# The mLSTM core with tokens on partitions

## Chip, cores and metric

The kernel runs on one core of a Trainium2 chip. The time is the device time of one execution in microseconds; before the change three runs gave 1299.15 to 1300.79 us, median 1299.8. A core has a matmul engine (PE, with PEld for its weight loads), a vector engine (DVE), a scalar engine (ACT), GpSimd (POOL) and a queue for DMA (SP). Each works through its own list of instructions in order; they meet only at semaphores.

## The reference, cut to what matters

A trunk of two layers on 512 tokens of width 1024 in float32. Layer 0 mixes tokens by latent attention, layer 1 by an mLSTM with 8 heads (query and key 64 wide, values 128 wide); behind each stands a squared-ReLU MLP of width 4096. The change touches only the mLSTM mixer:

```
qk   = silu(conv(u @ W_qk));  v = u @ W_v;  gate = sigmoid(u @ W_o_gate)
ig   = 15 tanh((i_pre + i_b) / 15);  lf = log_sigmoid(15 tanh((f_pre + f_b) / 15))
for each head, token t and earlier token s <= t:
    w[t, s]  = exp(b[t] - b[s] + ig[s] - m[t])        # b: running sum of lf, m: running maximum
    S[t, s]  = (q[t] . k[s]) / 8 * w[t, s]
    num[t]   = sum_s S[t, s] v[s]                     # 128 values
    den[t]   = sum_s S[t, s]                          # row sum
    h[t]     = num[t] / max(|den[t]|, exp(-m[t]))
    h[t]     = h[t] / sqrt(mean(h[t]^2) + 1e-6) * head_gain
mixer out = (gate * h) @ W_out
```

The kernel computes the chunkwise recurrence in this closed form. Division and norm fold into one factor per head and token: `(mean(num^2) + 1e-6 * dd^2) ^ -0.5`, with `dd` the maximum above.

## The kernel before, in words

Every large product is made in three passes. A float32 operand is split into a high half (`hi`, a cast to fp32r, by ACT) and a low half (`lo`, the rest, by DVE or POOL), and `product` (L1460 to L1469) issues hi*lo, hi*hi and lo*hi. Activations lie transposed, features on partitions and 512 tokens in the free dimension, as 8 tiles `xh`/`xl` and 8 tiles `uh`/`ul`. Weights come as strips of 1024 x 256 through two slots (`raw`, `whi`, `wlo`): SP loads, ACT casts (L636), DVE or POOL forms the low half (L963, L516), PE multiplies. Four PSUM banks rotate for dense tiles (`RING`, `free_bank`).

The order of the work is written out by hand for each engine; nothing plans it at run time. Layer 1 goes: gate rows, then four times a query/key strip and a value strip. The value strips (L1787 to L1797) already have the tokens stationary: 128 tokens by 256 columns, two halves to a bank. Then come four strips `N_O` of the output gate (tiles `T_O` to `T_O + 7`) in the transposed form, with `tile`: DVE scales a tile by the row of norms (`scaled`, L1361), ACT takes the sigmoid (L936), POOL multiplies the head gain into it (`gain`, L586).

The core follows, one head per step, software-pipelined over the engines. `i` and `lead` name a head by pair and parity; heads 3 to 6 stand in a loop (`Fori`) on each engine. For a head, with four blocks of key tokens j (512, 384, 256, 128 query columns, the causal triangle):

- DVE copies the head's 64 key rows into a zeroed 128-row buffer (`k_copy`, L1312) and adds the causal mask to the row of maxima (`masked`, L1322), which SP has brought into all partitions (`mb`).
- PE forms scores, key tokens on partitions (`st_product`, L1809); ACT the exponentials (`weights`, L859), seven instructions a head; DVE multiplies the two (`weighted`, L1330); ACT casts the result (`high`, L876), POOL forms its low half (`head_parts`, L563).
- PE forms the numerator, 128 value dimensions by 512 tokens (`numerator`, L1823), and in 8 more matmuls against two columns of ones the row sums in one row (`row_sums`, L1839).
- ACT squares the numerator (L886) and copies the row of sums (L892). PE adds the squares over partitions and turns the row of sums, both into columns (`head_sums`, L1848). DVE makes the norm's argument (`head_norm`, L1363), POOL raises it to -0.5 (`head_pow`, L573), DVE puts it on a diagonal (`head_diag`, L1379), PE spreads that over all partitions (`norm_spread`, L1862), DVE multiplies by the gate and by the numerator (`gated`, L1386).
- ACT casts and DVE forms the low half (L896, L1396) into `uh`/`ul`, the input of the output projection, whose first strip runs on PE beside the last heads (`out_products2`, L1868). Then come the other three strips and the MLP of layer 1.

Some steps have two buffers, by parity of the head or of the block. The halves of the scores (`swh`, `swl`) and of the values (`mvh`, `mvl`) lie in `xh` and `xl`, which the gate projection still reads.

Of the kernel before, what the change touches and what calls it, by code (L numbers as in the profile page):

```python
# [5 lines left out]
F32 = mybir.dt.float32  # L6
# [62 lines left out]
B_ST, B_NUM, B_BCH, B_DEN, B_STAT = 4, (3, 7), 0, 2, 6  # L69
# [30 lines left out]
def trunk(nc, a, out):  # L100
    ctx = ExitStack()
    with ctx:
# [42 lines left out]
        stat = sb("stat", [P, 2, 8])  # L145
        den_row = acc[0:1, :]
# [61 lines left out]
        sg = C("sg", [P, MH, S])  # L208
# [5 lines left out]
        rb = C("rb", [P, 2, S])  # L214
        mkh = C("mkh", [P, 2, S], F32R)
        mkl = C("mkl", [P, 2, S], F32R)
        numsq = rb
# [12 lines left out]
        otmp = yc  # L230
# [13 lines left out]
        mvh = flat(xh)[:, 3072:4096].rearrange("p (t n) -> p t n", t=TT)  # L244
        mvl = flat(xl)[:, 3072:4096].rearrange("p (t n) -> p t n", t=TT)


# [6 lines left out]
        def bank(b):  # L254
            return ps[:, b, :]

# [27 lines left out]
        sig_new, sg_ready = sem("sig_new"), sem("sg_ready")  # L284
# [3 lines left out]
        mk_zero, den_mm, den_read = sem("mk_zero"), sem("den_mm"), sem("den_read")  # L288
        md_ready, mk_ready, mv_hi, mv_lo = sem("md_ready"), sem("mk_ready"), sem("mv_hi"), sem("mv_lo")
        st_mm, w_exp, sw_mul, sw_hi, sw_lo = sem("st_mm"), sem("w_exp"), sem("sw_mul"), sem("sw_hi"), sem("sw_lo")  # L290
        num_mm, num_sq, ms_mm, stat_read = sem("num_mm"), sem("num_sq"), sem("ms_mm"), sem("stat_read")
        var2_ready, rc2_ready, diag2_ready = sem("var2_ready"), sem("rc2_ready"), sem("diag2_ready")
        bc2_mm, rb_ready, hs_ready = sem("bc2_mm"), sem("rb_ready"), sem("hs_ready")
# [182 lines left out]
        def _(pool):  # L476
# [86 lines left out]
            def head_parts(i, lead, early=False):  # L563

                for j in range(TT):
                    z = 4 * lead + j
                    pool.wait_ge(sw_hi, i * 8 + (z + 1))
                    g.tensor_tensor(swl(lead % 2, j), sw[:, z % 2, 0:LEN[j]], swh(lead % 2, j).bitcast(F32),  # L568
                                    ALU.subtract).then_inc(sw_lo, 1)
                    if j == 0 and not early:  # L570
                        head_pow(i, lead - 2)

            def head_pow(i, lead):  # L573
                c = slice(4 * (lead % 2), 4 * (lead % 2) + 4)
                pool.wait_ge(var2_ready, i * 2 + (lead + 1))
                g.tensor_tensor(rc2[:, c], var2[:, c], mhalf[:, 0:4], ALU.pow).then_inc(rc2_ready, 1)


            pool.wait_ge(y_lo, 8)
            for e in range(2):  # L580
                rows = slice(64 * (1 - e), 64 * (1 - e) + 64)
                g.memset(mkh[rows, e, :].bitcast(F32), 0.0)
                own.link(g.memset(mkl[rows, e, :].bitcast(F32), 0.0))
            g.nop().then_inc(mk_zero, 1)

            def gain(m):  # L586
                pool.wait_ge(sig_new, m + 1)
                g.tensor_scalar(sg[:, m, :], sg[:, m, :], pcol[:, G_HEAD + m:G_HEAD + m + 1], None, ALU.mult) \
                    .then_inc(sg_ready, 1)

            for m in range(7):
                gain(m)
            head_parts(0, 0, early=True)
            gain(7)
            head_parts(0, 1, early=True)
            head_parts(0, 2)
            with pool.Fori(1, MPAIRS - 1) as i:
                head_parts(i, 1)
                head_parts(i, 2)
            head_parts(MPAIRS - 1, 1)  # L600
            for lead in range(2):
                head_pow(MPAIRS - 1, lead)
# [7 lines left out]
        def _(act):  # L610
# [248 lines left out]
            def weights(i, lead, j):  # L859


                z, e, pair = 4 * lead + j, lead % 2, i + lead // 2
                fixed(act)
                if j == 0:
                    act.wait_ge(mb_in[e], pair * 16 + 16)
                    act.wait_ge(md_ready, i * 2 + (lead + 1))
                if z >= 2:
                    act.wait_ge(sw_mul, i * 8 + (z - 1))
                bias = gcol[:, ds(pair * 2 + (MH * j + e), 1)]
# [6 lines left out]
            def high(i, lead, j):  # L876

                z = 4 * lead + j
                act.wait_ge(sw_mul, i * 8 + (z + 1))
                sc.copy(swh(lead % 2, j), sw[:, z % 2, 0:LEN[j]]).then_inc(sw_hi, 1)  # L880

            def v_high(i, lead):
                e, pair = lead % 2, i + lead // 2
                sc.copy(mvh[:, :, P * e:P * e + P], v_tok[:, :, ds(pair * 256 + P * e, P)]).then_inc(mv_hi, 1)

            def square_num(i, lead):  # L886

                e = lead % 2
                act.wait_ge(num_mm, i * 2 + (lead + 1))
                sc.activation(numsq[:, e, :], bank(B_NUM[e]), ACT.Square).then_inc(num_sq, 1)  # L890

            def row_copy(i, lead):  # L892
                act.wait_ge(den_mm, i * 2 + (lead + 1))
                sc.copy(den_row, ps[0:1, B_DEN, :]).then_inc(den_read, 1)
# [8 lines left out]
            def head_step(i, lead, early=False, last=False):  # L903
# [4 lines left out]
                if not early:  # L908
                    gated_high(i, lead - 2)
# [1037 lines left out]
```

## Time and profile before

| | us |
|---|---|
| median of three runs | 1299.8 |
| the profiled execution | 1299.99 |
| its span, first to last instruction | 1298.2 |
| PE busy | 1231.2 (95%) |
| DVE busy | 675.5 (52%) |
| ACT busy | 455.1 (35%) |
| POOL busy | 281.1 (22%) |
| mean granted clock, share of full speed | 0.975 |

A row of a timeline gives the start and the length in us, the engine, the line, and in brackets the idle time before it with what ended it. A row of groups gives the summed and the mean time of instructions of one line and shape. `128*128` behind MATMUL is contraction rows by stationary columns, the shape behind it what is moved through. The granted clock is a share of 2.4 GHz; 0.5 is 1.2 GHz.

### The profile page before, as it was taken

How to read it: one execution, taken by the hardware profiler on the slowest of the kernel's cores; microseconds unless marked ns; L12 is line 12 of the kernel's file. 1: busy time of each engine (PE TensorE's matmuls, PEld its weight loads, DVE VectorE, ACT ScalarE, POOL GpSimd, SP SyncE). 2: the span in 40 equal slices, each digit the busy share in tenths (PEclk: the TensorE clock that was granted, in tenths of full speed). 3: DMA queues.
4: the chain of work that ended last, by engine and by line, in shares of the span. 5: the costliest groups of instructions: out<-in, count | busy, mean ns of one | idle time of the engine just before them, and what ended most of it. 6: DMA issues, size and time to landing. Idle time of an engine off the chain costs nothing.

```text
span 1298.2 us, 15828 instructions
## 1 busy us (share of the span) xinstructions
PE 1231.2 (95%) x5829; PEld 1016.0 (78%) x5829; DVE 675.5 (52%) x958; ACT 455.1 (35%) x725; POOL 281.1 (22%) x252
## 2 busy tenths in 40 slices
PE   6889999899999999999999998889999999999997
PEld 5667777678888888888889986676888888888885
DVE  6867888744533434434457544974443343343432
ACT  4336666543212212222343235652322221221232
POOL 4222222222201102002112134552220020110211
PEclk8999999899999999999999998988999999999998
DMA  5201011222233332232233331011323223223221
GB/s 159 60 22 28 23 26 25 94 68 94 97 98 97 98 97 97 97 97 97 67 99 99 113 97 47 27 41 38 99 91 102 94 97 100 94 97 97 97 66 65
DMA packets 113888, 104.00 MB, mean 80 GB/s; under 512 B 20935, under 2 KB 112165, under 8 KB 113837
## 3 DMA queue, kind: packets, MB, share of 16 engines
q1 hardware_dynamic: 113344, 102.98, 25.1%
q8 instruction: 35, 0.57, 0.2%
q10 hardware_dynamic: 492, 0.31, 0.1%
q14 instruction: 17, 0.13, 0.0%
HBM read 101.17 MB, written 2.11 MB: 80 GB/s over the span
## 4 chain that ended last, share of the span: by engine, by line
PE 79%; DVE 8%; issue 6%; ACT 3%; POOL 2%; ACTq 0%; DMA 0%; DVEq 0%; POOLq 0%
PE ps L1466 24%; PE ps L1468 24%; PE ps L1467 24%; DVE nmax L1109 2%; POOL xl L568 1%; DVE xl L968 1%; DVE qtmp L1101 1%; ACT prob L712 1%; ACT uh L726 1%; DVE rinv L1114 1%; ACT whi L636 1%; DVE diag L1382 1%; ACT xh L698 0%; PE ps L1716 0%; PE ps L1717 0%
## 5 line engine op out<-in xcount | busy, mean ns | idle before, releaser
L963 DVE TENSOR_TENSOR wlo<-raw,whi 128x2048 fp32r<-128x2048 f32 (+2 forms) x89 | 194.4, 2188 | 157.3 <-ACT whi L636 157.3
L1466 PE MATMUL ps<-xl,whi 128*128 128x512 f32 (+1 forms) x688 | 270.7, 393 | 3.2 <-DVE krot L1048 3.2
L636 ACT CAST whi<-raw 128x2048 fp32r<-128x2048 f32 (+4 forms) x150 | 184.7, 1259 | 246.3 <-PE ps L1468 237.7
L1467 PE MATMUL ps<-xh,whi 128*128 128x512 f32 (+1 forms) x688 | 268.5, 390 | 0.0
L1468 PE MATMUL ps<-xh,wlo 128*128 128x512 f32 (+1 forms) x688 | 268.3, 390 | 0.0
L1466 PE MATMUL ps<-ul,whi 128*128 128x512 f32 x608 | 237.2, 390 | 1.2 <-POOL wlo L516 1.2
L1468 PE MATMUL ps<-uh,wlo 128*128 128x512 f32 x608 | 236.6, 389 | 0.0
L1467 PE MATMUL ps<-uh,whi 128*128 128x512 f32 x608 | 236.5, 389 | 0.0
L546 POOL TENSOR_TENSOR ul<-sq,uh 128x512 fp32r<-128x512 f32 x64 | 83.7, 1309 | 521.1 <-ACT uh L815 521.1
L1191 DVE TENSOR_TENSOR h<-ps,h 128x512 f32<-128x512 f32 x80 | 55.0, 690 | 199.3 <-PE ps L1468 192.6
L1466 PEld LDWEIGHTS ps<-xl,whi 128*128 128x128 f32 (+1 forms) x688 | 128.9, 187 | 32.0 <-issue 4.9
L1467 PEld LDWEIGHTS ps<-xh,whi 128*128 128x128 f32 (+1 forms) x688 | 129.0, 188 | 28.1 <-issue 1.0
L1468 PEld LDWEIGHTS ps<-xh,wlo 128*128 128x128 f32 (+1 forms) x688 | 129.0, 187 | 27.7
L1466 PEld LDWEIGHTS ps<-ul,whi 128*128 128x128 f32 x608 | 114.1, 188 | 25.1 <-POOL wlo L516 1.6
L815 ACT CAST uh<-sq 128x512 fp32r<-128x512 f32 x64 | 39.7, 620 | 266.3 <-DVE sq L1222 266.3
L1468 PEld LDWEIGHTS ps<-uh,wlo 128*128 128x128 f32 x608 | 114.1, 188 | 23.8
L1467 PEld LDWEIGHTS ps<-uh,whi 128*128 128x128 f32 x608 | 114.2, 188 | 23.5
L1216 DVE TENSOR_TENSOR diag<-ps,r_a 128x512 f32<-128x512 f32 x64 | 44.0, 688 | 105.6 <-PE ps L1468 105.6
L504 POOL TENSOR_TENSOR acc<-acc,sq 128x512 f32<-128x512 f32 x38 | 53.0, 1395 | 159.5 <-ACT sq L650 159.1
L516 POOL TENSOR_TENSOR wlo<-raw,whi 128x64 fp32r<-128x64 f32 (+3 forms) x60 | 52.1, 895 | 132.1 <-ACT whi L636 132.1
L650 ACT ACTIVATE sq<-h 128x512 f32<-128x512 f32 x35 | 22.0, 630 | 89.3 <-DVE h L1191 88.1
L712 ACT ACTIVATE prob<-ps,nmax 128x128 f32<-128x128 f32 (+1 forms) x64 | 33.8, 529 | 55.1 <-DVE nmax L1109 55.1
(234 smaller groups left out, 1648.0 us busy)
## 6 DMA issues: line engine op xcount, KB each, us to landing
raw<-in_mlp_w SPq DMA_DIRECT2D x64, 1024.0 KB, 5.1
raw<-in_mlstm_w_in SPq DMA_DIRECT2D x12, 1024.0 KB, 5.3
raw<-in_mla_w_o SPq DMA_DIRECT2D x4, 1024.0 KB, 5.0
raw<-in_mlstm_w_o SPq DMA_DIRECT2D x4, 1024.0 KB, 5.0
raw<-in_mla_w_in SPq DMA_DIRECT2D x3, 1024.0 KB, 5.4
raw<-in_mla_w_uq SPq DMA_DIRECT2D x16, 192.0 KB, 2.5
x_tok<-in_x SPq DMA_DIRECT2D x4, 512.0 KB, 5.6
mb<-m_rows SPq DMA_DIRECT2D x8, 256.0 KB, 3.4
```

The costliest lines, as they stand in the source:

```text
L504: g.tensor_tensor(acc[:], acc[:], sq[:, k % 2, :], ALU.add).then_inc(acc_add, 1)
L516: last = g.tensor_tensor(lo, src, hi.bitcast(F32), ALU.subtract)
L546: g.tensor_tensor(ul[:, j, :], sq[:, j % 2, :], uh[:, j, :].bitcast(F32), ALU.subtract) \
L636: last = sc.copy(hi, src)
L712: sc.activation(prob[:, b % 2, 0:w], ps[:, B_S + b % 2, 0:w], ACT.Exp, bias=nmax[:, b:b + 1], accum_out=rsum[:, b:b + 1]).then_inc(s_exp, 1)
L815: sc.copy(uh[:, m, :], sq[:, m % 2, :]).then_inc(u_hi, 1)
L963: last = v.tensor_tensor(lo, src, hi.bitcast(F32), ALU.subtract)
L1191: return v.tensor_tensor(h[:, m, :], bank(t % RING), h[:, m, :], ALU.add)
L1216: v.tensor_tensor(diag[:, m % 2, :], bank((t0 + m) % RING), r_a[:], ALU.mult) \
L1466: mm(o, ah, bl, start=first, stop=False)
L1467: mm(o, ah, bh, start=False, stop=False)
L1468: ins = mm(o, al, bh, start=False, stop=last)
```

## The change

Layer 1's core turns round: tokens lie on partitions where value dimensions did.

- Output gate: the same form as the values' projection (`by_token`). ACT takes the sigmoid straight from PSUM with the token's norm as a scale per partition, 16 instructions of 256 columns. The gain leaves POOL.
- Scores: key and query rows of the head are used in place (64 rows, at partition 0 or 64); key copies and zeroed buffers go.
- Mask: POOL selects (`affine_select`, 128 x 512) from `mb`; two heads ahead of its use.
- Numerator: for query block b and key block j <= b the score block is stationary and the values are moved. The high values have two columns of ones beside them (130 wide), so column 128 of the result is the row sum. That is 30 matmuls a head; the two banks of a head hold four blocks of 256 columns. `row_sums`, `head_sums`, the row copy, the diagonal and the spread go.
- Squares: ACT squares, DVE reduces. Norm, power as before. `gated` is four instructions of 128 columns, each numerator * factor (per partition) * gate.
- The gated result is turned by four PE transposes; ACT casts it out of PSUM with the head gain as its scale, DVE forms the low half from there.
- All loops over heads are written out; the order of steps on each engine is new. SP's list stays as it is.

```diff
-B_ST, B_NUM, B_BCH, B_DEN, B_STAT = 4, (3, 7), 0, 2, 6
+B_ST, B_NUM, B_TURN = 1, (4, 6), (0, 3)
...
+        VW = P + 2
+        mvh = flat(xh)[:, 2560:2560 + 2 * TT * VW].rearrange("p (e t n) -> p e t n", e=2, t=TT)
...
+            def masked(u):          # POOL
+                pool.wait_ge(mb_in[u % 2], 16 * (u // 2) + 16)
+                if u >= 2:
+                    pool.wait_ge(w_exp, 4 * u - 4)
+                g.affine_select(out=blocks(md, u), in_=blocks(mb, u), compare_op=ALU.is_ge, fill=-NEG, base=0,
+                                pattern=[[0, TT], [1, P]], channel_multiplier=-1).then_inc(md_ready, 1)
...
+            def head_step(u):       # POOL
+                if u + 1 < MH:
+                    part_low(u + 1, 0)
+                    part_low(u + 1, 1)
+                if u >= 1:
+                    head_pow(u - 1)
+                if u + 2 < MH:
+                    masked(u + 2)
+                if u + 1 < MH:
+                    part_low(u + 1, 2)
+                    part_low(u + 1, 3)
+            masked(0)
+            pool.wait_ge(gemm_done, T_O + 8)
+            g.memset(mvh[:, :, :, P:VW].bitcast(F32), 1.0).then_inc(mv_one, 1)
+            for u in range(-1, MH + 1):
+                head_step(u)
             strip_low(N_WO2 + 1, "full")
...
+            def head_step(u):       # ACT
+                if u >= 1:
+                    square_num(u - 1)
+                if u + 1 < MH:
+                    high(u + 1, 0)
+                    weights(u + 1, 2)
+                    high(u + 1, 1)
+                if u >= 2:
+                    gated_high(u - 2)
+                if u + 1 < MH:
+                    v_high(u + 1)
+                    weights(u + 1, 3)
+                    high(u + 1, 2)
+                    if u + 2 < MH:
+                        weights(u + 2, 0)
+                    high(u + 1, 3)
+                    if u + 2 < MH:
+                        weights(u + 2, 1)
...
+                        last = sc.activation(sg[:, tt, 256 * j:256 * j + 256],
+                                             ps[:, t % RING, 256 * half:256 * half + 256],
+                                             ACT.Sigmoid, scale=rcol[:, tt:tt + 1])
...
+            def head_norm(u):       # DVE
+                c = slice(4 * (u % 2), 4 * (u % 2) + 4)
+                den = num(u)[:, :, P]
+                dve.wait_ge(num_sq, u + 1)
+                v.tensor_reduce(ssq[:, c], blocks(hs, u), op=ALU.add, axis=AX.X)
+                own.link(v.scalar_tensor_tensor(out=dd[:, c], in0=den, scalar=-1.0, in1=encol[:, 4 * u:4 * u + 4],
                                                 op0=ALU.mult, op1=ALU.max))
+                own.link(v.tensor_tensor(dd[:, c], den, dd[:, c], ALU.max))
                 own.link(v.scalar_tensor_tensor(out=dd[:, c], in0=dd[:, c], scalar=EPS, in1=dd[:, c],
                                                 op0=ALU.mult, op1=ALU.mult))
+                v.scalar_tensor_tensor(out=var2[:, c], in0=ssq[:, c], scalar=1.0 / P, in1=dd[:, c],
                                        op0=ALU.mult, op1=ALU.add).then_inc(var2_ready, 1)
+            def gated(u):
+                e = u % 2
+                dve.wait_ge(rc2_ready, u + 1)
+                for t in range(TT):
+                    last = v.scalar_tensor_tensor(out=hs[:, e, P * t:P * t + P], in0=num(u)[:, t, 0:P],
+                                                  scalar=rc2[:, 4 * e + t:4 * e + t + 1],
+                                                  in1=sg[:, t, P * u:P * u + P], op0=ALU.mult, op1=ALU.mult)
+                last.then_inc(hs_ready, 1)
+            def head_step(u):
+                if u + 1 < MH:
+                    weighted(u + 1, 0)
+                    weighted(u + 1, 1)
+                if u >= 1:
+                    head_norm(u - 1)
+                if u >= 2:
+                    gated_low(u - 2)
+                if u + 1 < MH:
+                    weighted(u + 1, 2)
+                    v_low(u + 1)
+                    weighted(u + 1, 3)
+                if u >= 1:
+                    gated(u - 1)
...
+            def numerator(u, bs):   # PE
+                e = u % 2
+                if 0 in bs:
+                    if u >= 2:
+                        pe.wait_ge(hs_ready, u - 1)
+                    pe.wait_ge(mv_lo, u + 1)
+                for b in bs:
+                    pe.wait_ge(sw_lo, 4 * u + b + 1)
+                    for j in range(b + 1):
+                        part = slice(P * (b - j), P * (b - j) + P)
+                        hi, lo, o = swh(e, j)[:, part], swl(e, j)[:, part], num(u)[:, b, :]
+                        mm(o[:, 0:VW], hi, mvh[:, e, j, :], start=(j == 0), stop=False)
+                        mm(o[:, 0:P], hi, mvl[:, e, j, :], start=False, stop=False)
+                        last = mm(o[:, 0:VW], lo, mvh[:, e, j, :], start=False, stop=(j == b))
+                if TT - 1 in bs:
+                    last.then_inc(num_mm, 1)
+            def turn_head(u):
+                pe.wait_ge(hs_ready, u + 1)
+                if u >= 2:
+                    pe.wait_ge(g_ready, u - 1)
+                for t in range(TT):
+                    part = slice(P * t, P * t + P)
+                    last = tr(ps[:, B_TURN[u % 2], part], hs[:, u % 2, part], ident[:])
+                last.then_inc(hs_turn, 1)
+            def head_step(u):
+                if u + 1 < MH:
+                    st_product(u + 1, 0)
+                    st_product(u + 1, 1)
+                if u >= 2:
+                    turn_head(u - 2)
+                numerator(u, (0, 1, 2))
+                if u + 1 < MH:
+                    st_product(u + 1, 2)
+                numerator(u, (3,))
+                if u + 1 < MH:
+                    st_product(u + 1, 3)
...
+            pe.wait_ge(sw_mul, 4 * MH)
+            out_products2(range(0, 3))
+            turn_head(MH - 2)
+            out_products2(range(3, 6))
+            turn_head(MH - 1)
+            out_products2(range(6, 8))
```

## Rows read from the trace of the kernel before

**Rows 1.** the page, busy time of the engines (us, share of the span, instructions)
```profile
PE 1231.2 (95%) x5829; PEld 1016.0 (78%) x5829; DVE 675.5 (52%) x958; ACT 455.1 (35%) x725; POOL 281.1 (22%) x252
```

**Rows 2.** windows cut at stages (from:to, us, busy us and instructions of each engine, granted clock)
```profile
753.60:799.40 45.80, 45.79 (x206) 37.71 (x204) 19.00 (x21) 18.18 (x21) 13.08 (x11) 1.00 0.24 75
799.40:807.31 7.91, 2.38 (x9) 1.64 (x10) 3.51 (x6) 6.37 (x13) 5.43 (x6) 0.81 0.00 0
807.31:866.30 58.99, 51.18 (x278) 40.18 (x278) 49.93 (x94) 36.74 (x90) 32.19 (x29) 0.88 0.13 41
...
866.30:899.85 33.55, 28.96 (x122) 21.45 (x120) 18.56 (x30) 8.41 (x16) 12.26 (x8) 0.80 0.10 32
```

**Rows 3.** timeline of PE, one head's scale spread and the next one's (start, length)
```profile
861.45 1.13 PE L1866 MATMUL ps<-diag,ones 128*128 128x512 f32 x2 [1.55 <-DVE diag L1382]
...
871.09 1.12 PE L1866 MATMUL ps<-diag,ones 128*128 128x512 f32 x2 [1.52 <-DVE diag L1382]
```

**Rows 4.** groups of DVE between 812 and 872 us (busy us, mean ns, idle before)
```profile
L1382 DVE TENSOR_TENSOR diag<-ident,rc 128x512 f32<-128x512 f32 x6 | 8.9, 1486 | 0.6 <-POOL rc L576 0.6
L1326 DVE TENSOR_TENSOR md<-mb,mask_w 128x512 f32<-128x512 f32 x6 | 4.6, 772 | 0.1
...
L1336 DVE SCALAR_TENSOR_TENSOR sw<-ps,wt 128x512 f32<-128x512 f32 x6 | 4.1, 685 | 1.2 <-PE ps L1468 1.2
L968 DVE TENSOR_TENSOR xl<-v_tok,xh 128x512 fp32r<-128x512 f32 x6 | 4.1, 683 | 0.0
...
L1390 DVE TENSOR_TENSOR rb<-ps,sg 128x512 f32<-128x512 f32 x5 | 3.4, 683 | 1.0 <-PE ps L1866 1.0
```

**Rows 5.** timeline of PE, matmuls by their width and at two clocks
```profile
185.54 0.60 PE L1605 MATMUL ps<-ident,prob 128*128 128x128 f32 x4
...
751.81 0.28 PE L1466 MATMUL ps<-wlo,xh 128*128 128x256 f32 x1
...
753.61 0.40 PE L1466 MATMUL ps<-xl,whi 128*128 128x512 f32 x1
...
850.12 0.41 PE L1466 MATMUL ps<-ul,mkh 128*128 x1
...
850.55 0.41 PE L1468 MATMUL ps<-uh,mkl 128*128 x1
...
867.91 0.27 PE L1466 MATMUL ps<-ul,mkh 128*128 x1
...
868.13 0.27 PE L1468 MATMUL ps<-uh,mkl 128*128 x1
```

**Rows 6.** groups of ACT between 812 and 872 us
```profile
L870 ACT ACTIVATE wt<-md,gcol 128x128 f32<-128x128 f32 x24 | 9.5, 396 | 5.7 <-DVE md L1326 5.5 <-issue 0.2
...
L872 ACT ACTIVATE wt<-mb,gcol 128x384 f32<-128x384 f32 x6 | 3.6, 600 | 0.0
```

**Rows 7.** timeline behind the gate projection, a table load of ACT
```profile
803.59 1.28 ACT L870 ACT_TABLE_LOAD   x1
```

**Rows 8.** groups of POOL between 812 and 872 us
```profile
L576 POOL TENSOR_TENSOR rc<-var,mhalf 128x4 f32<-128x4 f32 x6 | 8.7, 1447 | 2.9 <-DVE var L1376 2.9
L568 POOL TENSOR_TENSOR xl<-sw,xh 128x512 fp32r<-128x512 f32 x6 | 7.8, 1308 | 21.7 <-ACT xh L880 21.7
...
L568 POOL TENSOR_TENSOR xl<-sw,xh 128x384 fp32r<-128x384 f32 x6 | 6.0, 998 | 0.0
```

**Rows 9.** timeline of POOL, a small select, a pass over the gate, a strip pass
```profile
1.89 0.29 POOL L487 TENSOR_SCALAR_AFFINE_SELECT mask_s<-mask_s 128x128 f32<-128x128 f32 x1
...
804.10 1.56 POOL L588 TENSOR_SCALAR sg<-sg,pcol 128x512 f32<-128x512 f32 x1
...
885.52 4.54 POOL L516 TENSOR_TENSOR wlo<-raw,whi 128x2048 fp32r<-128x2048 f32 x1
```

**Rows 10.** timeline of DVE, the diagonal of the last two heads
```profile
876.73 0.69 DVE L1382 TENSOR_TENSOR diag<-ident,rc 128x512 f32<-128x512 f32 x1 [0.90 <-POOL rc L576]
...
885.59 5.03 DVE L1382 TENSOR_TENSOR diag<-ident,rc 128x512 f32<-128x512 f32 x1 [1.12 <-POOL rc L576]
```

More of the change, by code:

```diff
@@ L229, in trunk @@
         ys = E("ys", [P, 2, S])
-        otmp = yc
         def flat(t):
@@ L579, in _ @@
[L579 to L589, printed above, removed]
@@ L874, in weights @@
                 last.then_inc(w_exp, 1)
[L876 to L890, printed above, removed]
@@ L1424, in _ @@
-            v_low(0, 0)
-            weighted(0, 0, 2)
-            weighted(0, 0, 3)
-            for u in range(3):
-                if u == 2:
-                    dve.wait_ge(sg_ready, MH)
-                head_step(0, u, first=(u == 0), early=(u < 2))
-            with dve.Fori(1, MPAIRS - 1) as i:
-                own.enter(i, 1, 6)
-                head_step(i, 1)
-                head_step(i, 2)
-                own.leave(1, MPAIRS - 1)
-            head_step(MPAIRS - 1, 1, last=True)
-            gated(MPAIRS - 1, 0)
@@ L1443, in _ @@
+            for j in range(4):
+                split(N_O + j + 1)
+            head_step(-1)
+            dve.wait_ge(gemm_evac, T_O + 8)
+            for u in range(MH):
+                head_step(u)
+            head_norm(MH - 1)
+            gated(MH - 1)
+            gated_low(MH - 2)
+            gated_low(MH - 1)
             dve.wait_ge(wlo_ready, N_WO2 + 2)
@@ L1862, in norm_spread, with by_token @@
-            def norm_spread(i, lead, first=False):
-                pe.wait_ge(diag2_ready, i * 2 + (lead + 1))
-                if not first:
-                    pe.wait_ge(rb_ready, i * 2 + lead)
-                mm(bank(B_BCH), ones[:], diag[:, lead % 2, :], start=True, stop=True).then_inc(bc2_mm, 1)
+            def by_token(n, t0, j, i):
+                s, t = n % 2, t0 + 2 * j + i
+                free_bank(t)
+                for half in range(2):
+                    part = slice(P * (2 * i + half), P * (2 * i + half) + P)
+                    last = product(ps[:, t % RING, 256 * half:256 * half + 256],
+                                   [((xh[:, k, part], xl[:, k, part]), (full(whi[s])[:, k, :], full(wlo[s])[:, k, :]))
+                                    for k in range(8)])
+                last.then_inc(gemm_done, 1)
@@ new lines, in _, with st_product @@
+            for j in range(3):
+                strip_ready(N_O + j)
+                for i in range(2):
+                    by_token(N_O + j, T_O, j, i)
+            def st_product(u, j):
+                z, pair, e = 4 * u + j, u // 2, u % 2
+                if z >= 2:
+                    pe.wait_ge(sw_mul, z - 1)
+                rows, part = slice(64 * e, 64 * e + 64), slice(P * j, P * j + P)
+                kt = [x[rows, pair + 4, part] for x in (uh, ul)]
+                qt = [x[rows, pair, P * j:S] for x in (uh, ul)]
+                product(ps[:, B_ST + z % 2, 0:LEN[j]], [(kt, qt)]).then_inc(st_mm, 1)
```

351 lines of the change are left out of this document (84 added, 267 removed).

## The prediction

> **What bounds the kernel now.** The page comes first: the matmul engine is busy 95% of the span [rows 1], so time is to be had only where it waits. The windows come next, cut at the ends of stages [rows 2]. While the output gate is projected (753.6 to 799.4 us) PE never stops. In the 7.9 us after it PE works 2.4 us. Over the six middle heads (807.3 to 866.3 us) PE shows 51.2 of 59.0 us, DVE 49.9; the mean clock of 0.88 means that (1 - 0.88) / 0.5 of these 59 us, 14 us, ran at the lower level (1.2 GHz), where a matmul lasts twice as long. In the last stretch (to 899.85, where the second weight strip of the output projection starts) PE waits 4.6 us and the clock of 0.80 makes 13 us at the lower level. So the cell's core and its two edges are 100.45 us, from the last gate matmul to that strip; what lies behind is dense matmul work, which neither gains nor loses by the change.
>
> Inside the core PE's timeline shows the period: the matmul pair that spreads a head's scale over the partitions starts at 861.45 and at 871.09 us, 9.64 us apart, each time after 1.5 us of waiting for DVE's diagonal [rows 3]. What fills DVE stands in its groups [rows 4]: diagonal 1.49 us, mask 0.77, two gating multiplies of 0.68, the weightings, the values' low half. The chain of a head is head sums, norm, power, diagonal, spread, gate, weighting, and DVE stands in it four times.
>
> **The gate's projection** turns from 24 matmuls of 512 columns a tile to 48 of 256. Before: 192 of them and the 12 score matmuls of head 0 fill 45.8 us [rows 2]. With 0.228 us for 512 columns the scores of a head (three each of 512, 384, 256 and 128 columns, the last not under 0.11) are 1.9 us, which leaves 43.8 us for the 192, 0.228 each. After: the value projection already has the new form; 15 of its matmuls lie between 751.81 and 753.61 us [rows 5], 0.12 us each, and 384 make 46.1 us. PE is the bound here, so **+2.3 us**, and nothing hides it. ACT takes the tiles out of PSUM itself with 16 sigmoids of 256 columns, between the 0.40 us of 128 and the 0.60 of 384 columns [rows 6]; DVE's eight multiplies and POOL's eight gains go. A tile lasts 5.8 us and needs 1.0 us of ACT, a strip's cast lies beside it; were ACT late, three more banks stand between it and a wait of PE.
>
> **The start.** The heads' halves overwrite the rows that the gate projection reads, so ACT can start only at its end, as before. From there: two sigmoids 1.0, cast of part 0 0.5, the table load for the exponential 1.3 [rows 7], exponentials of part 2 and cast of part 1 to 4.0, values 4.5; POOL's low half of part 1 to 5.0 and head 1's mask to 6.0; then, on ACT, exponentials of head 1 and its first cast to 8.5. Before, POOL began the first low half of head 1 at 807.31, 7.91 us after the gate's end; now 8.5: **+0.6 us**. Ends: -1 us if the mask finds POOL free, +2 us if ACT is held once more.
>
> **One head, engine by engine.**
> DVE: four weightings, by columns from the 0.69 of 512, 1.9 us; the new sum of the squares, no less than a 128-column pass (0.28) and no more than the diagonal (1.49), taken as one 512-column pass, 0.7; four small operations 0.2 each when free, some held by POOL, 1.6; low half of the result 0.7; values 0.7; four gatings of 128 columns with one operand from PSUM, 1.1. Together 6.7 us of a period. Diagonal, mask, two key copies and one gating pass are gone.
> ACT: seven exponentials, four casts, values, squares, gated half: 6 us; the copy of the row sums is gone.
> PE: scores 1.9 us, as before (64 rows of contraction instead of 128 leave the columns as they are). The numerator is now 30 matmuls with 128 stationary and 128 or 130 moving columns. Three of 128x128 in a row come every 0.11 us at full clock (867.91 and 868.13, two apart), every 0.215 at half (850.12 and 850.55) [rows 5]: 3.3 or 6.4 us. They replace 20 matmuls of up to 512 columns, eight for the squares, four small turns and the spread pair (1.1 us [rows 3]). Four transposes add at most 0.6 [rows 5]. PE needs 5.7 us a head at full clock, 10.5 at half.
> POOL: low halves 1.31, 1.0 and, by columns, 1.2 and 0.7, together 4.2; power 1.45 [rows 8]; and, new, the mask of 128x512. No such mask is in the trace. From below: the 128x128 select, 0.29 us; from above: POOL's 512-column pass over the gate, 1.56 [rows 9]. I take 1.0, four of the small ones less their overlap, because it is the same instruction. POOL: 6.65 us.
>
> **What closes the loop.** POOL becomes the fullest, and it is tied to ACT by the order of the two: low halves 0 and 1, power, mask (1.31 + 1.0 + 1.45 + 1.0 = 4.76); then ACT's exponentials for the next head's part 0 (0.8), which wait for that mask and stand ahead of the cast of this head's part 3 (0.2); its second pair of exponentials (0.75); the squares of the last numerator (0.55); the next head's first cast (0.6); and POOL again, with hops 0.1. Sum 7.8 us. The spread was late before; the mask is late next.
> To it comes the lock of DVE and POOL. The diagonal, whose two inputs lie in SBUF, took 0.69 us at 876.73 and 5.03 us from 885.59 [rows 10], when POOL's strip pass of 4.54 us had just begun at 885.52 [rows 9]. The gatings and the low half of the result now read one operand from PSUM, as the 0.68 us multiply of rows 4, whose mean shows no such stretch. Still exposed are the third and fourth small operation and the values' low half; the latter meets the power or the mask, and the weighting of part 3 is queued behind it, for which PE's next scores and ACT's cast wait. The cost lies between 0 and the 0.7 of a whole values pass; I add 0.3: **8.1 us a head**.
> The page "SBUF — State Buffer" of the Trainium skill, section "Who interferes with whom", says that a DVE instruction with two SBUF inputs and a GpSimd instruction that reads SBUF exclude each other for the whole instruction. By that rule, the trace agrees; with it the loop is 8.1, and if the rule did not hold it would be 7.8, 1.5 us less over five heads.
>
> Middle: the first step has no power and no squares, 6.6 us; five more at 8.1: 47.1 us, against 59.1 before (from POOL's first low half of head 1 to that of head 7). **-12.0 us.** With the mask at its lower or upper end (0.3, 1.6) five heads give -15.5 or -9.
>
> **The clock.** Before, the half-clock stretch in the middle cost little, for PE was not the bound; now PE needs 10.5 us for a head that takes 8.1. PE was busy 51.2 of 59.0 us; now 5.7 of 8.1 us is 70% at full clock, with one or two gaps a head as before. I expect one stretch of about a head's length in the middle: **+2.5 us**; the ends are 0 and 14 us (all at half).
>
> **The tail.** From the first low half of head 7: its second one, the power of head 5 and low halves 2 and 3 to 5.7 us; gating and turning of head 5 and the last numerator to 8.8; then 18 products of the projection (4.1), the turn of head 6, 18 more, while head 7's squares, sum, power and gating are done (4.9 us behind its numerator); turn of head 7, cast, low half, last products: 21 us. Before: 33.4 us, with 4.6 us of PE idle [rows 2], most of it because the diagonal was held 4.3 us by the strip pass, and with 13 us at half clock. The power of head 7 still stands ahead of that pass in POOL's queue, and nothing of head 7 behind it has two SBUF inputs. I add 3 us for one half-clock stretch on the path: 24 us. **-9.4 us.**
>
> **Sum.** 2.3 + 0.6 - 12.0 + 2.5 - 9.4 = -16.0 us. The profiled execution took 1299.99 us (span 1298.2 and 1.8 around it), 0.2 above the median of the runs: **1284 us.**
>
> **Rivals.**
> *The clock stays at half through the heads.* PE at 70% with a gap in each head could be too little. For it: every window behind the gate has a stretch at the lower level. Against: 0.88, not 0.5, over the middle, at nearly this share. Price: six heads at 10.5 are 63 us, 13.4 more than my 49.6, and the tail's numerator and products at half add 4: 1301.5 us, slower than before. It decides once PE's head (10.5) is over the old period of 9.64. 8%.
> *POOL's mask is dear.* Each us of it is in the loop. At 3 us, twice the pass over the gate, it adds 2 us in six heads: 1296. Against: 0.29 for the small one. 12%.
> *The loop is loose.* If the mask hides and no half-clock stretch falls on the path, only POOL's own 6.65 us and the wait for one weighting and cast beside its last low half remain (0.69 + 0.6 - 0.7), 7.25 a head: -4.5, and -5.5 for the clock: 1274. 15%.
> *The change moves nothing*: the sums on DVE were waited for by nobody, and ACT, POOL and DVE take turns in the new order as they did in the old one, 9.6 us a head. Then the middle gives back 9 us and the tail half of its gain: 1298. 5%. Against: no engine of the new order sums to more than 6.7 us.
>
> **Numbers.** My forecast has 60%, its own range 1277 to 1292. The range of all: 1272 to 1297. About 0.2% (2.6 us) is what can be told from no change. Faster 0.87, same 0.05, slower 0.08.
>
> **What would show it.** Heads 8.1 us apart on PE instead of 9.64; a gate projection of 46.1 us without idle; on POOL a mask of 1.0 us and a share over 80% in the middle; ACT's first exponential of a head waiting for that mask; numerator matmuls every 0.11 us; the second strip 82 to 84 us behind the gate's end. Wrong would make it: a mask over 2 us, numerator matmuls slower than those of rows 5, or a mean clock under 0.75 in the middle.

## The result and the profile after

| | before | after |
|---|---|---|
| median of 20 runs each, us | 1298.6 | 1305.5 |
| range, us | 1289.1 to 1302.1 | 1301.3 to 1308.0 |
| span of the profiled execution, us | 1298.2 | 1304.9 |
| mean granted clock | 0.975 | 0.953 |

The ratio is 1.0062, 95% interval 1.0048 to 1.0075: slower by 0.6%, where 1284 us, faster by 16, had been forecast.

The page of the changed kernel: busy time, and the granted clock in 40 slices of 33 us.

```profile
PE 1252.8 (96%) x6021; PEld 1051.4 (81%) x6021; DVE 645.7 (49%) x934; ACT 452.5 (35%) x725; POOL 263.3 (20%) x249
...
PEclk8899999999999999999999998557999999999998
```

DVE and POOL have less to do than in [rows 1], and PE is busy for 21.6 us longer. The two fives in the clock's line stand where the core of the mLSTM is. The windows, cut at the ends of stages like [rows 2] (the last scaling of a value tile, which in the kernel before stands at 753.81 us, the last gate matmul, POOL's first low half of head 1 and of head 7, the second strip of the output projection):

```profile
755.11:802.60 47.49, 47.49 (x390) 46.90 (x388) 11.20 (x8) 18.63 (x25) 0.00 (x0) 1.00 0.21 67
802.60:811.27 8.67, 5.45 (x22) 4.00 (x20) 2.95 (x5) 7.34 (x17) 4.58 (x7) 0.68 0.11 32
811.27:875.29 64.02, 64.02 (x268) 56.54 (x267) 34.49 (x80) 33.03 (x83) 29.25 (x36) 0.50 0.12 37
875.29:905.69 30.40, 28.80 (x127) 25.42 (x126) 12.39 (x35) 7.97 (x14) 11.07 (x8) 0.68 0.11 35
```

In the third row PE is busy for 64.02 of 64.02 us, and the clock is 0.50 throughout, 1.2 GHz. DVE is down from 49.9 to 34.5 us, and that is worth nothing, because DVE, ACT and POOL now all wait for PE. The same core in windows of 10 us:

```profile
790.00:800.00 10.00, 10.00 (x78) 9.47 (x78) 3.45 (x3) 7.31 (x11) 0.00 (x0) 1.00 0.00 1
800.00:810.00 10.00, 6.78 (x37) 5.27 (x36) 1.85 (x4) 6.11 (x14) 4.21 (x6) 0.78 0.08 24
810.00:820.00 10.00, 10.00 (x43) 8.75 (x42) 3.10 (x6) 5.55 (x15) 4.38 (x6) 0.50 0.09 30
...
880.00:890.00 10.00, 8.58 (x40) 8.28 (x40) 5.28 (x17) 1.89 (x4) 2.20 (x3) 0.50 0.00 0
890.00:900.00 10.00, 10.00 (x44) 8.53 (x44) 3.12 (x10) 3.07 (x3) 5.41 (x2) 0.78 0.01 2
900.00:910.00 10.00, 9.82 (x46) 7.82 (x44) 2.82 (x4) 4.69 (x6) 1.55 (x2) 1.00 0.32 106
```

The clock falls in the pause behind the gate projection and rises again only at 894 us, among the first 512-column matmuls of the output projection; all windows between show 0.50. PE's timeline has the turns of two heads 11.01 us apart, with no idle time in brackets, and behind each the numerator's matmuls, one every 0.21 us. The first row shows PE's wait behind the gate projection:

```profile
806.79 0.76 PE L1393 MATMUL ps<-ul,uh 64*128 64x512 f32 x1 [3.22 <-DVE sw L1306]
...
841.21 1.12 PE L1785 MATMUL ps<-ident,hs 128*128 128x128 f32 x4
841.97 0.46 PE L1772 MATMUL ps<-xh 128*128 128x130 f32 x1
842.23 0.41 PE L1773 MATMUL ps<-xl,xh 128*128 128x128 f32 x1
842.44 0.42 PE L1774 MATMUL ps<-xh,xl 128*128 128x130 f32 x1
842.66 0.41 PE L1772 MATMUL ps<-xh 128*128 128x130 f32 x1
...
852.22 1.11 PE L1785 MATMUL ps<-ident,hs 128*128 128x128 f32 x4
```

Stage by stage in the two profiled executions: ahead of the gate +1.3 us; the gate's stretch 45.6 to 47.5, +1.9; start 7.9 to 8.7, +0.8; middle 59.1 to 64.0, +4.9; tail 33.4 to 30.4, -3.0; behind the second strip's start 398.3 to 399.2, +0.9. Together +6.8, the difference of the spans is 6.7. The first and the last stretch hold the same instructions in both kernels.

### The profile page after: what moved, and what is told of

The parts are those of the page before. It is cut to its first block, busy times and chain, and to the rows that moved or that the text cites. A ratio compares the mean times of both kernels' runs of the same rounds, so it can differ in the third digit from the quotient of the medians.

```text
span 1304.9 us, 15951 instructions
## 1 busy us (share of the span) xinstructions
PE 1252.8 (96%) x6021; PEld 1051.4 (81%) x6021; DVE 645.7 (49%) x934; ACT 452.5 (35%) x725; POOL 263.3 (20%) x249
## 4 chain that ended last, share of the span: by engine, by line
PE 84%; DVE 7%; issue 4%; ACT 3%; POOL 1%; ACTq 0%; DMA 0%; DVEq 0%; POOLq 0%
PE ps L1393 25%; PE ps L1395 25%; PE ps L1394 24%; DVE nmax L1097 2%; PE ps L1772 1%; PE ps L1774 1%; PE ps L1773 1%; DVE xl L956 1%; DVE qtmp L1089 1%; ACT prob L711 1%; ACT uh L725 1%; PE ps L1643 1%; PE ps L1785 1%; DVE rinv L1102 1%; ACT whi L635 1%
## 5 line engine op out<-in xcount | busy, mean ns | idle before, releaser
L1393 PE MATMUL ps<-xl,whi 128*128 128x512 f32 (+1 forms) x624 | 246.1, 394 | 3.2 <-DVE krot L1036 3.2
L1394 PE MATMUL ps<-xh,whi 128*128 128x512 f32 (+1 forms) x624 | 243.8, 391 | 0.0
L1395 PE MATMUL ps<-xh,wlo 128*128 128x512 f32 (+1 forms) x624 | 243.6, 390 | 0.0
L1393 PEld LDWEIGHTS ps<-xl,whi 128*128 128x128 f32 (+1 forms) x624 | 117.1, 188 | 29.6 <-issue 4.9
L1394 PEld LDWEIGHTS ps<-xh,whi 128*128 128x128 f32 (+1 forms) x624 | 117.2, 188 | 25.7 <-issue 1.0
L1395 PEld LDWEIGHTS ps<-xh,wlo 128*128 128x128 f32 (+1 forms) x624 | 117.1, 188 | 25.4
L1393 PE MATMUL ps<-wlo,xh 128*128 128x256 f32 x256 | 72.5, 283 | 0.0
L1394 PE MATMUL ps<-whi,xh 128*128 128x256 f32 x256 | 72.4, 283 | 0.0
```

Source lines behind the costliest of these rows:

```text
L1393: mm(o, ah, bl, start=first, stop=False)
L1394: mm(o, ah, bh, start=False, stop=False)
L1395: ins = mm(o, al, bh, start=False, stop=last)
```

## The experiments

The theory: the heads' work on PE no longer brings the clock back once it has fallen, though PE never waits; at the lower clock PE is the bound, so nothing else counts. The rivals: the clock merely stays where the pause has put it, and a filled pause would do; or PE is slow for another reason and the loop of POOL and ACT would be no faster than forecast anyway. Every ratio is against runs of the kernel before on the same chip, with its 95% interval. "Middle" is again from POOL's first low half of head 1 to that of head 7.

**Filling the pause (s_fill).** 14 matmuls of 128x512 on the output projection's first strip, into a free bank, between the scores of head 0 and its numerator:

```diff
+            def fill(b, n):
+                for _ in range(n):
+                    mm(ps[:, b, :], whi[N_WO2 % 2][:, 0:P], whi[N_WO2 % 2][:, 0:S], start=True, stop=True)
...
+            pe.wait_ge(gemm_evac, T_O + 7)
+            strip_ready(N_WO2)
+            fill(3, 14)
```

> Adds 14 matmuls of 512 columns behind the gate projection, into a free bank, so that PE's pause before the first numerator is filled; nothing else changes. Theory G (the gap lets the clock fall, and only a head that starts at half stays there): the heads run at full clock, 8 us apart, 1282 to 1287 us. Theory N (the heads' own narrow matmuls do not hold the full clock, wherever they start): the clock falls in the first heads and stays at half, 11.0 us apart, 1301 to 1306 us.

Measured: 1297.3 us, ratio 0.9988 (0.9970 to 1.0006). Windows:

```profile
800.00:810.00 10.00, 9.45 (x55) 7.44 (x54) 2.96 (x5) 8.26 (x20) 5.54 (x7) 1.00 0.11 26
810.00:820.00 10.00, 9.27 (x63) 7.46 (x63) 7.65 (x17) 6.91 (x19) 8.08 (x10) 1.00 0.15 52
820.00:830.00 10.00, 10.00 (x45) 9.19 (x45) 6.45 (x14) 6.27 (x18) 5.23 (x7) 0.50 0.08 29
```

Neither range was met: the time lies between them. The pause no longer drops the clock, which is worth 8 us, but at 820 us, 15 us behind the fillers, it falls all the same, with PE busy for 9.27 of the 10 us before, and stays down to the projection. The pause is one occasion of the fall, not the only one.

**Wide matmuls in every head too (sh_fill4).** The same, and four more ahead of each head's transposes:

```diff
             def turn_head(u):
...
+                fill(B_TURN[u % 2], 4)
                 for t in range(TT):
```

> As s_fill, and four matmuls of 512 columns ahead of each head's transposes, 0.9 us of PE a head at full clock and 1.7 at half. Theory N: wide matmuls in each head hold the full clock for most of the stretch, 8.0 to 8.7 us a head, 1283 to 1292 us although PE does more. Theory O (the order of ACT, DVE and POOL sets 11 us whatever the clock): full clock, but still about 11 us a head, 1301 us or more. If four are too few, half clock and 12.7 us a head, 1316 us.

Measured: 1284.3 us, ratio 0.9882 (0.9852 to 0.9912). From the third head on a head carries 1 us more of PE work, and the middle takes 43.8 us instead of 64.0, at a mean clock of 0.96; the one dip, 3.4 us long, is at 820 to 824 us, where two unfilled heads are over and the first filled one begins. The profiled execution was the fastest of the five (1278.3 us, clock 0.987; the others took 1283.9 to 1285.0 at 0.982 to 0.985), so these windows show a somewhat better case than the median.

**A wide numerator (wide_num).** The values are stationary and the scores are moved, in 13 matmuls of up to 512 columns instead of 30 narrow ones; 64-row scores stay.

```diff
-                        mm(o[:, 0:VW], hi, mvh[:, e, j, :], start=(j == 0), stop=False)
-                        mm(o[:, 0:P], hi, mvl[:, e, j, :], start=False, stop=False)
-                        last = mm(o[:, 0:VW], lo, mvh[:, e, j, :], start=False, stop=(j == b))
...
+                    o = ps[:, B_NUM[e], P * b:S]
+                    mm(o, mvh[:, e, b, 0:P], swh(e, b), start=(b == 0), stop=False)
+                    mm(o, mvl[:, e, b, :], swh(e, b), start=False, stop=False)
+                    last = mm(o, mvh[:, e, b, 0:P], swl(e, b), start=False, stop=(b == TT - 1))
+                    if b == 0:
+                        last = mm(ps[:, B_NUM[e] + 1, :], mvh[:, e, b, 0:P], swh(e, b), start=True, stop=True)
```

> The numerator's 30 matmuls of 128 or 130 columns become 13 of up to 512 columns, values stationary and scores moved, with every wait left as it is; the numerator is then not turned and the row sums are not formed. Theory N: the clock is at full for most of the heads, as before the change, 7.8 to 8.5 us a head, 1280 to 1290 us. If the narrow form is not what holds the clock down: half clock, PE 8.6 us a head, 1288 to 1292 us with a mean clock near 0.5 in the heads.

Measured: 1275.0 us, ratio 0.9805 (0.9773 to 0.9836). That is faster than both ranges. Its middle takes 42.1 us at a mean clock of 0.86, falling and rising as before the change. The heads also need less of PE than the narrow form (8.6 us at half clock by the estimate above, where the changed kernel's take 11.0), so not all of the gain is the clock's:

```profile
810.78:852.89 42.11, 37.21 (x171) 29.01 (x170) 35.56 (x80) 32.31 (x83) 30.69 (x35) 0.86 0.20 57
```

**Scores over 128 rows again (k128).** The numerator as changed, and nothing filled:

```diff
-                rows, part = slice(64 * e, 64 * e + 64), slice(P * j, P * j + P)
+                rows, part = slice(0, P), slice(P * j, P * j + P)
```

> The scores contract over 128 rows (both heads of the pair together) instead of 64; columns and waits stay. The scores are then those of two heads summed. Theory R (64 idle rows of the array keep the clock down): full clock in the heads, about 8.1 us a head, 1282 to 1288 us. Theory N: no change, half clock, 11.0 us a head, 1304 to 1307 us.

Measured: 1281.9 us, ratio 0.9866 (0.9835 to 0.9896). The number and the columns of PE's matmuls are those of the changed kernel, the new transposes included, so these are not what holds the clock down. The pause drops the clock here as well, but the heads bring it back, and then PE has time to spare:

```profile
810.00:820.00 10.00, 10.00 (x59) 9.71 (x58) 4.93 (x11) 5.55 (x15) 5.02 (x7) 0.67 0.07 26
820.00:830.00 10.00, 8.82 (x65) 7.59 (x63) 8.83 (x23) 7.10 (x19) 7.65 (x9) 1.00 0.16 55
...
840.00:850.00 10.00, 8.08 (x62) 7.17 (x61) 9.31 (x20) 7.31 (x19) 8.02 (x10) 1.00 0.47 133
...
860.00:870.00 10.00, 10.00 (x39) 9.16 (x39) 3.62 (x13) 3.07 (x3) 2.57 (x3) 0.50 0.01 2
```

So a PE that is less busy (8 of 10 us) held 2.4 GHz, where one that was busy all the time stayed at 1.2. The rule that the clock follows PE's busy time fails here.

**128 rows with the missing ones zero (k128z).** Zeroed buffers, filled once before the heads, so that no head pays for copies; the later heads use the keys of the first two:

```diff
...
-                kt = [x[rows, pair + 4, part] for x in (uh, ul)]
-                qt = [x[rows, pair, P * j:S] for x in (uh, ul)]
+                kt = [x[:, e, part] for x in (mkh, mkl)]
+                qt = [x[:, pair, P * j:S] for x in (uh, ul)]
```

> Scores over 128 rows with keys in a padded buffer filled once (heads 0 and 1 for all others) whose other 64 rows are zero; no copies in the heads. It differs from k128 in the zeros alone. If rows of zeros count like others: as k128, 1280 to 1284 us, 7.3 us a head at full clock. If zeros do not count: half clock through the heads, 1302 to 1306 us, and pad was slower than k128 for that and not for its copies.

Measured: 1281.1 us, ratio 0.9873 (0.9843 to 0.9902), the same as k128, and its clock is up again as early, at 817 us. In this pair rows of zeros hold the clock as well as rows of numbers:

```profile
820.00:830.00 10.00, 8.87 (x65) 7.65 (x65) 8.90 (x22) 6.94 (x18) 7.75 (x9) 1.00 0.15 55
```

**Fillers of 64 rows (sh_fill4_r64).** As sh_fill4, but the heads' fillers contract over 64 rows. They last as long: four take 2.07 us at half clock (at 846.42 us), as four of 128 rows do.

```diff
+                    mm(ps[:, b, :], whi[N_WO2 % 2][0:rows, 0:P], whi[N_WO2 % 2][0:rows, 0:S], start=True, stop=True)
...
+            fill(3, 14, P)
```

> sh_fill4 with the four wide matmuls of each head contracting over 64 rows instead of 128; the 14 at the start stay at 128. Theory W (columns moved count, whatever the rows): as sh_fill4, 1278 to 1286 us. Theory R: half the rows count half, the clock falls to half in the heads and stays, PE then needs 12.7 us a head, 1305 to 1315 us; if two full ones were enough, it stays up and this reads as W.

Measured: 1310.7 us, ratio 1.0099 (1.0064 to 1.0134): 26 us over sh_fill4, from the rows alone. Windows of sh_fill4_r64:

```profile
820.00:830.00 10.00, 9.68 (x41) 8.06 (x39) 6.76 (x15) 6.06 (x16) 6.09 (x9) 0.60 0.15 49
830.00:840.00 10.00, 10.00 (x41) 8.47 (x41) 5.54 (x13) 4.93 (x12) 4.63 (x6) 0.50 0.03 10
```

and of sh_fill4:

```profile
820.00:830.00 10.00, 9.75 (x54) 8.14 (x55) 7.77 (x17) 7.65 (x20) 5.59 (x8) 0.83 0.12 29
830.00:840.00 10.00, 9.76 (x74) 8.45 (x72) 8.85 (x21) 8.19 (x21) 7.56 (x8) 1.00 0.08 26
```

**64 rows in the kernel before (before_r64).** The loops of PE written out, the scores over 64 rows, into which DVE now copies the keys of either head:

```diff
...
-                    qt = [x[:, ds(pair, 1), P * j:S].rearrange("p a s -> p (a s)") for x in (uh, ul)]
-                    product(o, [((mkh[:, e, part], mkl[:, e, part]), qt)]).then_inc(st_mm, 1)
+                    qt = [x[0:64, ds(pair, 1), P * j:S].rearrange("p a s -> p (a s)") for x in (uh, ul)]
+                    product(o, [((mkh[0:64, e, part], mkl[0:64, e, part]), qt)]).then_inc(st_mm, 1)
```

> The kernel before with only the contraction of its scores cut to 64 rows (keys of both heads in rows 0 to 63, queries of the even head for both, so the odd heads' scores are not theirs) and PE's loop written out. Columns, waits and the other engines' work stay. Theory R: the clock is at half for more of the middle than before (mean under 0.7 there against 0.88), 1303 to 1320 us. Theory that rows matter only together with the narrow numerator: within 3 us of the kernel before, mean clock there 0.85 or more.

Measured: 1297.5 us, ratio 1.0001 (0.9982 to 1.0019). Its middle, 59.5 us at 0.86, is that of [rows 2] (59.0 at 0.88). The smaller scores alone do no harm while the numerator, the squares and the spread are wide; they do it together with the narrow numerator. Either of the two undone, in wide_num or in k128, kept the clock from staying down.

**Padded keys as a repair (pad, pad_start).** POOL copies a head's key rows into zeroed 128-row buffers, between two low halves; pad_start also fills the pause.

```diff
+            def k_copy(u):          # POOL
+                rows = slice(64 * (u % 2), 64 * (u % 2) + 64)
...
+                own.link(g.tensor_copy(mkh[rows, u % 2, :], uh[rows, u // 2 + 4, :].bitcast(F32)))
+                g.tensor_copy(mkl[rows, u % 2, :], ul[rows, u // 2 + 4, :].bitcast(F32)).then_inc(mk_ready, 1)
...
+                kt = [x[:, e, part] for x in (mkh, mkl)]
+                qt = [x[:, pair, P * j:S] for x in (uh, ul)]
```

> The scores contract over 128 rows again, against keys in a buffer whose other 64 rows are zero, as before the change, but copied by POOL (two copies of 64x512 a head, estimated 0.65 us each from the 0.64 us mask), everything else as in the changed kernel. Theory R (the rows of the array that a matmul occupies count, whatever lies in them): full clock for most of the heads, 7.3 to 7.8 us a head, 1280 to 1285 us. If rows of zeros do not count: half clock, 11 us a head, 1305 us.

> pad, and 14 wide matmuls in the pause behind the gate projection. Theory R: as pad without the half clock of the first heads, 3 to 5 us less, 1276 to 1281 us. If the start has no part in it: as pad.

Measured: pad 1294.6 us, ratio 0.9985 (0.9968 to 1.0001); pad_start 1292.8, ratio 0.9965 (0.9948 to 0.9983). Both missed: I had thought the copies hidden. In pad PE waits for them three times, 1.68, 3.07 and 2.40 us from 847 us on:

```profile
847.66 0.47 PE L1414 MATMUL ps<-ul,mkh 128*128 128x512 f32 x1 [1.68 <-POOL mkl L582]
```

The middle takes 58.7 us at a mean clock of 0.67. k128z, which differs in the copies and their wait alone, is 14 us faster, so these are what the repair costs. The waits explain only part of it. Before them, until 842 us, the clock stands at 0.50 although PE has scores over all 128 rows and hardly a gap (0.12 us in 10):

```profile
820.00:830.00 10.00, 9.88 (x43) 9.34 (x42) 5.38 (x15) 4.87 (x13) 5.99 (x9) 0.50 0.07 26
```

In k128z the same matmuls brought the clock back at 817 us. So 128 rows in the scores are not always enough; why they were not in pad is open.

**Fillers where PE is ahead (fill_e4, fill_e6).** Against sh_fill4 the place changes: the fillers stand before the wait for the gated result and not behind it, where they had come on top of it, and the first two heads, which turn nothing, have them too. The two were not tried apart. fill_e6 takes six instead of four.

```diff
+                if u >= 4:
+                    pe.wait_ge(g_ready, u - 3)
+                fill(B_TURN[u % 2], 4)
                 if u >= 2:
                     turn_head(u - 2)
```

> Four wide matmuls of 128 rows in each of the eight head steps, issued before PE waits for the gated head instead of behind that wait, and the 14 at the start. Theory R/N (the heads' own array work is just too little, added wide work holds the clock): full clock from the start to the tail, 7.3 us a head, the fall at 820 us of sh_fill4 gone, 1276 to 1281 us. If the place of the filling does not matter: as sh_fill4, 1284 us.

> The same with six a head, 1.4 us of PE at full clock. If four are enough, six cost what PE has no room for (7.1 of 7.3 us), 1277 to 1284 us, level with fill_e4 or up to 3 us above; if four leave stretches at half, six are faster by 2 to 6 us.

Measured: fill_e4 1273.7 us, ratio 0.9818 (0.9792 to 0.9844); fill_e6 1278.6, ratio 0.9853 (0.9827 to 0.9879). fill_e4 is 2 us below its range, fill_e6 is within its own but 4.9 us above fill_e4 instead of at most 3. Windows of fill_e4, cut as above:

```profile
755.15:802.65 47.50, 47.50 (x390) 46.91 (x388) 11.20 (x8) 18.63 (x25) 0.00 (x0) 1.00 0.21 68
802.65:811.34 8.69, 8.13 (x43) 6.22 (x41) 2.96 (x5) 7.36 (x17) 4.64 (x6) 1.00 0.13 30
811.34:853.72 42.38, 42.38 (x295) 35.59 (x294) 35.79 (x80) 32.44 (x83) 31.17 (x35) 1.00 0.17 57
853.72:875.24 21.52, 21.04 (x125) 17.75 (x125) 12.40 (x35) 7.99 (x14) 11.09 (x8) 1.00 0.15 49
```

Gate and start are those of the changed kernel to 0.02 us, the clock is 1.00 in all four, and the whole gain lies in the last two rows: 64.02 - 42.38 = 21.6 and 30.40 - 21.52 = 8.9 us, together 30.5 of the 31.6 between the spans. This kernel computes all of the reference and beats both others. In fill_e6 the heads' fillers start 7.67 us apart, where fill_e4's are 7.2 apart: PE has become the bound at full clock, and each further wide pair costs its own time.

**Heads' fillers alone (e4_nostart).**

```diff
-            pe.wait_ge(gemm_evac, T_O + 7)
             strip_ready(N_WO2)
-            fill(3, 14)
```

> fill_e4 without the 14 matmuls behind the gate projection. If the filled heads alone can raise the clock once it has fallen: half clock for the first 10 to 15 us of the heads, where PE needs 12.7 us a head, then full; 2 to 5 us above fill_e4, 1276 to 1279 us. If they can only hold it, not raise it (as s_fill's fall and the changed kernel's 85 us at half could be read): half clock to the end, 12.7 us a head, 1310 us or more.

Measured: 1286.2 us, ratio 0.9904 (0.9887 to 0.9921), 12.5 us over fill_e4. Windows:

```profile
800.00:810.00 10.00, 6.78 (x27) 4.88 (x25) 2.95 (x5) 7.94 (x19) 5.18 (x7) 0.67 0.08 28
810.00:820.00 10.00, 10.00 (x42) 8.75 (x43) 2.13 (x5) 3.87 (x11) 3.40 (x5) 0.50 0.08 26
820.00:830.00 10.00, 10.00 (x42) 9.15 (x43) 3.74 (x8) 3.52 (x9) 4.58 (x5) 0.50 0.08 26
830.00:840.00 10.00, 10.00 (x56) 7.86 (x54) 7.59 (x20) 6.48 (x17) 5.34 (x7) 0.79 0.12 29
840.00:850.00 10.00, 10.00 (x71) 8.56 (x71) 9.13 (x23) 8.16 (x21) 6.62 (x8) 1.00 0.08 26
```

The heads' fillers do raise the clock, as expected, but the price was missed: it took them more than two heads, until the window from 830 us, and a filled head at half clock is longer than an unfilled one. Its fillers, on PE's timeline:

```profile
807.80 2.07 PE L1780 MATMUL ps<-whi 128*128 128x512 f32 x4
819.77 2.07 PE L1780 MATMUL ps<-whi 128*128 128x512 f32 x4
831.74 2.07 PE L1780 MATMUL ps<-whi 128*128 128x512 f32 x4
```

They are 11.97 us apart, where the changed kernel's heads are 11.01. The middle takes 54.2 us instead of 42.4. In sh_fill4 a dip of 3.4 us ended with the first fillers, here one of 31 us (803 to 834) took three sets of them; why they differ is open. What is shown is that fillers which keep the clock from falling in the pause are worth more than those that raise it later.

## Why the prediction was wrong

**The step that failed is the clock.** It was one term of +2.5 us, for a single half-clock stretch in the middle, with 14 us as its upper end, and 3 us in the tail. The reason given was PE's busy share (70%, as before) and its gaps. Both were the wrong thing to look at: the clock stayed at half while PE was busy 100% of the time and held full speed in k128 at 80%. Against fill_e4, whose clock is not down in these stages, the term is 21.6 us in the middle and 8.9 in the tail. The 21.6 is more than the upper end of 14, because the loop that a fallen clock has to exceed is itself shorter than forecast, 7.3 us a head and not 8.1. The text had the right alternative, the clock that stays at half, with a price for the middle that came out (63 us forecast, 64.0 measured) and too small a one for the tail (28 forecast, 30.4 measured), and gave it 8%. The price for the middle was in part luck. The text's own terms at half clock, twice 1.9 us for the scores, 6.4 for the numerator and up to 1.2 for the transposes, come to as much as 11.4 a head and not 10.5. Measured were 11.01, but the first two steps took only 9.45 and 10.52. What should have raised that chance was in its own arithmetic: a head of 10.5 us at half clock over a loop of 8.1 means that a fallen clock has no slack to be hidden in, and the change took away exactly PE's wide work over 128 rows, which the text counted only as time saved.

The text held that 64 rows of contraction instead of 128 change nothing ("leave the columns as they are"). For the time of a matmul that is right: a 64-row filler lasts as long as a 128-row one. What they do to the clock was not weighed at all. The page "TensorE: Matmul & The Clock Gate" of the Trainium skill, section "The HAM clock gate", puts the clock down to how busy PE has been; by that rule a PE without a gap would have been back at 2.4 GHz. The third window of the changed kernel (64.02 of 64.02 us busy at 0.50) does not agree, and the measurement decides.

**Gate projection, +2.3: right.** The stretch is 47.5 us with six score matmuls (1.3 us) in it, 46.2 for the 384; forecast 46.1. PE has no idle time in it.

**Start, +0.6: right.** 8.7 us against 8.5. The table load took 1.28 us again, and ACT's order was as counted.

**The loop of POOL and ACT, 8.1 us a head: the mechanism right, the size 0.8 us off.** In the changed kernel it is hidden behind PE. At full clock, in k128, the turns come every 7.32 us:

```profile
836.92 0.66 PE L1785 MATMUL ps<-ident,hs 128*128 128x128 f32 x4 [0.25 <-DVE hs L1333]
...
844.24 0.66 PE L1785 MATMUL ps<-ident,hs 128*128 128x128 f32 x4 [0.25 <-DVE hs L1333]
```

and the loop can be read off POOL's timeline and ACT's:

```profile
839.09 2.26 POOL L576 TENSOR_TENSOR xl<-sw,xh 128x512 fp32r<-128x512 f32 x2 [1.24 <-ACT xh L877]
841.44 1.01 POOL L582 TENSOR_TENSOR rc<-var,mhalf 128x4 f32<-128x4 f32 x1
842.42 1.04 POOL L570 TENSOR_SCALAR_AFFINE_SELECT md<-mb 128x512 f32<-128x512 f32 x1
...
846.40 2.25 POOL L576 TENSOR_TENSOR xl<-sw,xh 128x512 fp32r<-128x512 f32 x2 [1.24 <-ACT xh L877]
```

```profile
843.54 0.40 ACT L867 ACTIVATE wt<-md,gcol 128x128 f32<-128x128 f32 x1 [0.74 <-POOL md L570]
...
845.24 0.58 ACT L887 ACTIVATE hs<-ps 128x512 f32<-128x512 f32 x1
845.72 0.61 ACT L877 CAST xh<-sw 128x512 fp32r<-128x512 f32 x1
```

Low halves, power and mask end at 843.46, ACT's first exponential waits for the mask, and its cast releases POOL at 846.40: 4.37 + 0.08 + 2.79 + 0.07 = 7.31 us. Forecast for the same steps: 4.76, 2.9 and hops, 7.8, and 0.3 for the lock. The power took 1.01 instead of 1.45. The mask took 1.04, as forecast (1.0), but by luck: alone it is 0.64, and the lock, which had its own 0.3, makes up the rest.

**The tail, -9.4 (24 us): the work right, the clock not.** At full clock, in fill_e4, it is 21.5 us; forecast 21, and 3 for the clock. Measured 30.4, with a mean clock of 0.68.

**Sum.** The span of 1304.9 us is 22.7 over the forecast one (1284 less the 1.8 around it): middle 14.4, tail 6.4, start 0.2, gate stretch -0.4 (+1.9, which with the 0.7 of scores moved behind it is +2.6, against 2.3 counted for the projection alone), and 1.3 and 0.9 in stretches that the change does not touch.

**Settled and open.** Shown: the lower clock in the heads is the loss (fill_e4, sh_fill4), the pause is one occasion of its fall (s_fill, e4_nostart), and whether it holds depends on wide work and full rows, not on busy time alone (wide_num, k128, k128z against the changed kernel; sh_fill4_r64 against sh_fill4). Open: how much of each the chip wants, why full rows did not bring the clock back in pad, and why the clock in s_fill falls at 820 us and not sooner. The kernel before is itself not free of the loss: its middle shows 0.88.

## What to carry to other kernels

Work out PE's time per round at half clock beside the round's period: where it is the longer, the clock decides the sign of the change and needs a term for the whole stage. Wide matmuls over all 128 rows that a change removes (sums by ones, spreads, zero padding) may have been what held the clock. Count them as such and not only as time saved. A few unused wide matmuls at a point where PE is ahead, and some in the pause before, cost little here (1 us of PE a head) and were worth 31.7 us between the medians of 1305.5 and 1273.7.

## What the runs showed of the hardware

- The granted clock did not follow PE's busy time: 85 us at 1.2 GHz with one gap, of 1.4 us near 885 (changed kernel, about 809 to 894 us), and 2.4 GHz at 80% busy (k128).
- Rows of zeros did as much for the clock as rows of numbers (k128z 1281.1, k128 1281.9 us), but in pad, with zero rows too, it stayed at 1.2 GHz for 36 us with PE busy for 99% of them; 64 rows instead of 128 leave a matmul's time alone and cost 26 us by the clock (sh_fill4_r64).
- A 128x512 select on POOL takes 0.64 us beside PE and ACT alone, and 1.04 beside DVE's low half of the values, which reads two operands from SBUF. The page "SBUF — State Buffer" of the Trainium skill, section "Who interferes with whom", has these two exclude each other, and the trace agrees. DVE's last two small operations on 4 columns show the same: 0.64 and 0.93 us instead of 0.15. Groups of DVE and POOL in the changed kernel between 812 and 874 us, to be read beside [rows 4] and [rows 8]:

```profile
L1325 DVE SCALAR_TENSOR_TENSOR var<-ssq,dd 128x4 f32<-128x4 f32 x5 | 4.6, 928 | 0.2
...
L1323 DVE SCALAR_TENSOR_TENSOR dd<-dd 128x4 f32<-128x4 f32 x5 | 3.2, 642 | 0.2
```

```profile
L582 POOL TENSOR_TENSOR rc<-var,mhalf 128x4 f32<-128x4 f32 x5 | 5.1, 1011 | 0.5
...
L570 POOL TENSOR_SCALAR_AFFINE_SELECT md<-mb 128x512 f32<-128x512 f32 x6 | 3.8, 639 | 0.0
```
